# Banded attention of a streaming-encoder block: groups of 32 queries in place of transposes of the probabilities

## The reference, cut to what matters

```python
x = x + 0.5 * swiglu(rms_norm(x, ff1_norm), ...)          # d_ff 2816
proj = rms_norm(x, mix_norm) @ w_in                       # q 8 heads x 64, k and v 2 heads x 64, u 512
# attention: chunk n (64 queries) sees keys of chunks n-1 and n (128 keys)
scores = q @ k_win.T * 64 ** -0.5 - slope[head] * |qi - kj|
m = max(max(scores), sink[head])
p = exp(scores - m);  p = p / (sum(p) + exp(sink[head] - m))
attn = p @ v_win
ssm = s5_ssm_glu(u, ...)                                  # state space group, GELU, GLU
x = x + concat(rms_norm(attn), rms_norm(ssm)) @ w_out
x = x + 0.5 * swiglu(rms_norm(x, ff2_norm), ...);  out = rms_norm(x, final_norm)
```

## Time and profile before

| what | value |
|---|---|
| median of 3 runs (lowest, highest) | 1579.27 us (1579.03, 1579.45) |
| the profiled execution's own time | 1579.26 us |
| its span in the trace | 1577.6 us |
| mean granted TensorE clock | 0.999 |
| PE, DVE, ACT, POOL busy | 1568.1, 1104.8, 708.1, 533.0 us |

### The profile page before, as it was taken

One profiled execution on the slowest core, in us unless ns is written; L12 is line 12 of the kernel. 1 busy time (PEld: TensorE's weight loads), 2 busy tenths in 40 slices (PEclk: granted clock), 3 DMA queues, 4 the chain that ended last, 5 costly groups with the idle time before them and its releaser, 6 DMA issues.

```text
span 1577.6 us, 21967 instructions
## 1 busy us (share of the span) xinstructions
PE 1568.1 (99%) x7481; PEld 1295.2 (82%) x7481; DVE 1104.8 (70%) x1740; ACT 708.1 (45%) x1305; POOL 533.0 (34%) x986
## 2 busy tenths in 40 slices
PE   9999999999999999999999999999999999999998
PEld 7888888888888888878887888888888888888887
DVE  7966677666579887864368768765666666588767
ACT  7543434343434445421567544444444434344444
POOL 4228888877567778323130240000000000002000
PEclk9999999999999999999999999999999999999999
DMA  8363334333488555777631141333333333886444
GB/s 289 97 85 111 109 130 139 131 134 135 154 322 266 153 136 138 222 227 177 137 120 41 54 160 50 111 107 108 107 107 107 107 107 129 315 276 180 121 111 170
DMA packets 164311, 231.89 MB, mean 147 GB/s; under 512 B 26856, under 2 KB 100464, under 8 KB 160752
## 3 DMA queue, kind: packets, MB, share of 16 engines
q1 hardware_dynamic: 159728, 222.07, 44.2%
q0 software_dynamic: 4320, 8.41, 3.0%
q10 hardware_dynamic: 160, 0.07, 0.0%
HBM read 154.26 MB, written 75.20 MB: 145 GB/s over the span
## 4 chain that ended last, share of the span: by engine, by line
PE 99%; DMA 0%; ACT 0%; issue 0%; DVE 0%; SPq 0%; DVEq 0%; ACTq 0%
PE bank L1209 31%; PE bank L1211 31%; PE bank L1210 31%; PE bank L1552 1%; PE bank L1579 1%; PE bank L1534 1%; PE bank L1505 0%; PE bank L1565 0%; PE bank L1527 0%; DMA x_in<-in_x_dram 0%; PE bank L1243 0%; PE bank L1427 0%; PE bank L1235 0%; PE bank L1431 0%; PE bank L1428 0%; PE bank L1714 0%
## 5 line engine op out<-in xcount | busy, mean ns | idle before, releaser
L1209 PE MATMUL bank<-hbhi,ws_lo 128*128 128x512 f32 x1040 | 405.1, 390 | 0.0
L1211 PE MATMUL bank<-hbhi,ws_hi 128*128 128x512 f32 x1040 | 404.7, 389 | 0.0
L1210 PE MATMUL bank<-hblo,ws_hi 128*128 128x512 f32 x1040 | 404.6, 389 | 0.0
L1211 PEld LDWEIGHTS bank<-hbhi,ws_hi 128*128 128x128 f32 x1040 | 195.2, 188 | 40.9
L1209 PEld LDWEIGHTS bank<-hbhi,ws_lo 128*128 128x128 f32 x1040 | 195.2, 188 | 40.7 <-issue 0.4
L1210 PEld LDWEIGHTS bank<-hblo,ws_hi 128*128 128x128 f32 x1040 | 195.2, 188 | 40.2
L1209 PE MATMUL bank<-d_hi,ws_lo 128*128 128x512 f32 x572 | 222.7, 389 | 0.0
L1211 PE MATMUL bank<-d_hi,ws_hi 128*128 128x512 f32 x572 | 222.5, 389 | 0.0
L1210 PE MATMUL bank<-d_lo,ws_hi 128*128 128x512 f32 x572 | 222.5, 389 | 0.0
L1836 ACT ACTIVATE loc<-bank 128x512 f32<-128x512 f32 x160 | 96.0, 600 | 252.0 <-PE bank L1211 252.0
L1883 ACT ACTIVATE d_hi<-d_in 128x512 fp32r<-128x512 f32 x154 | 96.5, 631 | 202.6 <-DMA d_in<-b_scratch 202.5
(11 more groups left out here) (320 smaller groups left out, 2710.7 us busy)
## 6 DMA issues: line engine op xcount, KB each, us to landing
b_scratch<-loc SPq DMA_DIRECT2D x42, 1024.0 KB, 7.3
d_in<-b_scratch SPq DMA_DIRECT2D x154, 256.0 KB, 3.4
raw2a<-in_ff_w_up_dram SPq DMA_DIRECT2D x42, 512.0 KB, 4.8
loc<-in_ff_w_gate_dram SPq DMA_DIRECT2D x36, 512.0 KB, 5.1
xT<-x_scratch SPq DMA_DIRECT2D x12, 1024.0 KB, 7.7
x_scratch<-xT SPq DMA_DIRECT2D x5, 2048.0 KB, 8.1
dw_lo_place<-in_ff_w_down_dram SPq DMA_DIRECT2D x8, 1024.0 KB, 7.3
x_in<-in_x_dram SPq DMA_DIRECT2D x8, 512.0 KB, 7.8
```

The lines of the kernel that those rows point to most:

```text
L1209: nc.tensor.matmul(o, wl, rh, start=first, stop=False, skip_group_check=chain)
L1210: nc.tensor.matmul(o, wh, rl, start=False, stop=False, skip_group_check=chain)
L1211: return nc.tensor.matmul(o, wh, rh, start=False, stop=last, skip_group_check=chain)
```

## The change

- The partition axis of scores and probabilities is now four groups of 32 queries, one per chunk: a step m takes four chunks and half of the heads. `S` has 32 matmuls (64 rows, 32 columns, 128 keys moving), eight in a round: four column groups times two row halves.
- The sink is column 129 of each row of `sco`, written by POOL before the scores (`set_sinks`). The maximum runs over 129 columns, and so do the exponentials and their sums; the sink's own instructions are gone on DVE and ACT.
- `B` is the reciprocal alone. POOL multiplies by it (128x1024). `t` on DVE transposes the blocks of 32x32 into one buffer `pts` (two instructions of 128x512). T and C are gone.
- `V` has 32 matmuls: 32 keys (four row groups, one per chunk), 64 columns (two column groups, one per key/value head), 128 moving columns, four accumulated products each; chunk a goes to bank 2 + a. `O` copies from four banks in one instruction.
- `sco` has three buffers, numbered in the semaphore counts by `sinks_number` (m + 1 up to m = 2, then 2m - 1) and `scaled_number` (2m + 4 up to m = 5, then m + 9). The p steps have two banks in place of three. The order tables are rewritten; V7 stands right ahead of n0, which now waits for O7, and n1 stands behind p15.
- v goes through DRAM: 4 DMAs into `vt_scratch`, a wait on the SP queue, 16 DMAs into `vwin`. The bias is loaded by 16 DMAs behind the four `xT` loads, where one DMA in the state-space part loaded it.
- The injection I2 moves from projection (7, 1) to the start of projection (8, 0), nine matmuls of 128x512 later.

The diff, cut to what the text speaks of:

```diff
 WITH_PE = {(1, 1): steps("m1"), (6, 0): steps("K0"), (6, 1): steps("I0"),
-           (7, 0): steps("I1"), (7, 1): steps("I2"),
+           (7, 0): steps("I1"), (8, 0): steps("I2"),
            (10, 0): steps("Y0 I3"), (10, 1): steps("Y1"), (11, 1): steps("Y2"), (12, 0): steps("Y3")}
...
-ATT_PE = steps("P0 P1 S2 p2 T0 p3 T1 V0 S3 p4 V1 S4 T2 p5 T3 V2 S5 p6 V3 S6 p7 T4 p8 T5 V4 S7 p9 V5 p10 T6 p11 T7 V6 V7 p12 n0 p13 r0 p14 n1 p15")
-ATT_ACT = steps("W13 X0 X1 C0 C1 O0 X2 X3 O1 C2 W14 C3 O2 X4 O3 X5 W15 C4 C5 O4 X6 s0 s1 X7 O5 C6 s2 s3 q0 C7 O6 W16 O7 s4 s5 s6 s7 n0 W17 h0 h1 h2 h3 n1 W18 h4 h5 h6 h7 W19")
-ATT_DVE = steps("A0 A1 B0 p0 p1 B1 A2 W13 A3 B2 p2 p3 B3 p4 A4 W14 p5 A5 p6 B4 p7 B5 A6 W15 p8 A7 B6 p9 B7 p10 a0 W16 p11 j5 g0 j6 n0 j7 p12 W17 p13 h0 h1 h2 h3 p14 g1 p15 W18 n1 h4 h5 h6 h7 W19")
+ATT_PE = steps("P0 P1 p2 S2 p3 S3 p4 V0 S4 p5 V1 S5 p6 V2 p7 S6 V3 p8 S7 V4 p9 p10 V5 p11 V6 p12 V7 n0 p13 p14 r0 p15 n1")
+ATT_ACT = steps("W13 W14 X0 X1 X2 O0 W15 X3 O1 X4 O2 X5 O3 s0 X6 O4 X7 W16 s1 O5 s2 W17 O6 s3 O7 q0 n0 s4 s5 s6 s7 h0 h1 h2 h3 n1 W18 h4 h5 h6 h7 W19")
+ATT_DVE = steps("W13 A0 p0 A1 p1 W14 B0 p2 A2 t0 B1 A3 B2 p3 t1 A4 p4 B3 p5 t2 A5 t3 B4 p6 p7 A6 t4 B5 p8 A7 B6 t5 W15 p9 B7 p10 t6 W16 t7 p11 a0 p12 g0 W17 n0 j5 p13 j6 p14 h0 h1 j7 h2 h3 g1 p15 n1 W18 h4 h5 h6 h7 W19")
...
-SSM_BANK = [6, 7, 5]
-V_BANK = [4] * 7 + [0]
+SSM_BANK = [7, 6]
+V_BANK = [2, 3, 4, 5]
...
+def sinks_number(m):
+
+    return m + 1 if m < 3 else 2 * m - 1
+
+
+def scaled_number(m):
+
+    return 2 * m + 4 if m < 6 else m + 9
...
-    nm = small("nm", [P, 2, 8])
-    esk = small("esk", [P, 2, 8])
-    ssum = small("ssum", [P, 2, 8])
-    rden = small("rden", [P, 8])
...
             sp.wait_ge(pads_set, 1)
-            vt = vTp[:, :].rearrange("p (n c i) -> p n c i", c=2, i=32)
-            for c in range(4):
+            for d in range(4):
+                sp.dma_start(vt_d[:, :, 32 * d:32 * d + 32].rearrange("n j i -> j n i"),
+                             vTp[32 * d:32 * d + 32, :].rearrange("j (n i) -> j n i", i=32)).then_inc(v_loaded, 16)
+            sp.wait_ge(v_loaded, 4 * 16)
+            for a in range(4):
+                for n in range(4):
+                    c = 8 * n + 2 * a
+                    sp.dma_start(vwin[32 * a:32 * a + 32, n, :, :],
+                                 vt_d[c:c + 4, :, :].rearrange("b j d -> j b d")).then_inc(v_loaded, 16)
+
+        def load_bias():
+            sp.wait_ge(glu_done, 8)
+            sp.wait_ge(y_ready, 8)
+            for b in range(4):
                 for a in range(4):
-                    sp.dma_start(vwin[32 * c:32 * c + 32, :, 32 * a:32 * a + 32],
-                                 vt[32 * a:32 * a + 32, c // 2:c // 2 + 16, c % 2, :]).then_inc(v_loaded, 16)
+                    sp.dma_start(biast[32 * a:32 * a + 32, b, :, :, :].rearrange("p v g k -> p (v g k)"),
+                                 bias_c[32 * b:32 * b + 32].rearrange("i v k -> i (v k)")).then_inc(side_loaded, 16)
 
...
                 if h:
-                    pe.wait_ge(mix_taken, 14)
+                    pe.wait_ge(mix_taken, 15)
                 else:
-                    pe.wait_ge(pt_taken, 16)
+                    pe.wait_ge(o_taken, 8)
             elif norm == N_FF2 and h == 0:
...
                 pe.wait_ge(pads_set, 1)
-            for nn in range(2):
-                n = 2 * m + nn
-                for a in range(2):
+            for gl in range(2):
+                for qh in range(2):
+                    for a in range(4):
+                        n = 4 * (m // 2) + a
+                        for kv in range(NKV):
+                            r = slice(kv * HD, (kv + 1) * HD)
+                            o = bank[kv][32 * a:32 * a + 32, (2 * gl + qh) * P:(2 * gl + qh + 1) * P]
+                            last = nc.tensor.matmul(o, qT[r, n, 2 * (m % 2) + gl, 32 * qh:32 * qh + 32],
+                                                    kTp[r, n * CHUNK:n * CHUNK + P], start=True, stop=True,
+                                                    skip_group_check=True)
+                            if gl == qh == 1 and a == 3:
+                                last.then_inc(s_ready, 1)
+
+        def weighted(m):
+            if m:
+                pe.wait_ge(o_taken, m)
+            else:
+                pe.wait_ge(v_loaded, 20 * 16)
+                pe.wait_ge(h_tmp, split_before(N_ATT))
+            pe.wait_ge(p_turned, 2 * m + 2)
+            for b in range(4):
+                for a in range(4):
+                    k = slice(32 * a, 32 * a + 32)
                     for kv in range(NKV):
-                        r = slice(kv * HD, (kv + 1) * HD)
-                        o = bank[kv][:, (2 * nn + a) * P:(2 * nn + a + 1) * P]
-                        last = nc.tensor.matmul(o, qT[r, n, 2 * a:2 * a + 2, :].rearrange("p g q -> p (g q)"),
-                                                kTp[r, n * CHUNK:n * CHUNK + P], start=True, stop=True)
-                        if nn == a == 1:
-                            last.then_inc(s_ready, 1)
-
-        def transposes_p(m):
-            pe.wait_ge(p_done, m + 1)
-            if m:
-                pe.wait_ge(pt_taken, 2 * m)
-            for kv in range(NKV):
-                for nn in range(2):
-                    for a in range(2):
-                        o = bank[2 + kv][:, (2 * nn + a) * P:(2 * nn + a + 1) * P]
-                        last = nc.tensor.transpose(o, sco[m % 2][:, kv, nn, a, :], ident[:, :])
-                last.then_inc(pt_ready, 1)
-
-        def weighted(m):
-            if m == 7:
-                pe.wait_ge(s_biased, 16)
-            elif m:
-                pe.wait_ge(o_taken, m)
-            else:
-                pe.wait_ge(v_loaded, 16 * 16)
-                pe.wait_ge(h_tmp, split_before(N_ATT))
-            pe.wait_ge(pt_taken, 2 * m + 2)
-            for nn in range(2):
-                for kv in range(NKV):
-                    last = nc.tensor.matmul(bank[V_BANK[m]][kv * HD:(kv + 1) * HD, nn * 256:(nn + 1) * 256],
-                                            vwin[:, 2 * m + nn, kv * HD:(kv + 1) * HD],
-                                            pts[m % 2][:, kv, nn, :, :].rearrange("p a q -> p (a q)"),
-                                            start=True, stop=True)
+                        d = slice(kv * HD, (kv + 1) * HD)
+                        last = nc.tensor.matmul(bank[V_BANK[a]][d, 0:P], vwin[k, m // 2, b, d],
+                                                pts[k, kv, :, b, :], start=b == 0, stop=b == 3,
+                                                skip_group_check=True)
             last.then_inc(o_ready, 1)
 
         def ssm_piece(i, between=None):
...
             act.wait_ge(max_done, m + 1)
-            for s in range(8):
-                kv, nn, a = s // 4, s // 2 % 2, s % 2
-                v = sco[m % 2][:, kv, nn, a, :]
-                act.activation(v, v, ACT.Exp, bias=nm[:, m % 2, s:s + 1], scale=1.0,
-                               accum_out=ssum[:, m % 2, s:s + 1])
-            act.activation(esk[:, m % 2, :], esk[:, m % 2, :], ACT.Exp).then_inc(exp_done, 1)
-
-        def p_out(m):
-            for kv in range(NKV):
-                act.wait_ge(pt_ready, 2 * m + kv + 1)
-                if m >= 2:
-                    act.wait_ge(o_ready, m - 1)
-                else:
-                    act.wait_ge(h_tmp, split_before(N_ATT))
-                act.activation(pts[m % 2][:, kv, :, :, :].rearrange("p n a q -> p (n a q)"), bank[2 + kv][:, :],
-                               ACT.Copy).then_inc(pt_taken, 1)
+            for c in range(8):
+                v = sco[m % 3][:, c, :]
+                last = act.activation(v, v, ACT.Exp, bias=nm[:, m % 3, c:c + 1], scale=1.0,
+                                      accum_out=ssum[:, m % 3, c:c + 1])
+            last.then_inc(exp_done, 1)
 
         def o_out(m):
 
             act.wait_ge(o_ready, m + 1)
-            act.activation(qT[:, 2 * m:2 * m + 2, :, :].rearrange("p n g q -> p (n g q)"), bank[V_BANK[m]][:, :], ACT.Copy
-                           ).then_inc(o_taken, 1)
+            n = 4 * (m // 2)
+            act.activation(qT[:, n:n + 4, 2 * (m % 2):2 * (m % 2) + 2, :].rearrange("p n g q -> p n (g q)"),
+                           banks[:, V_BANK[0]:V_BANK[3] + 1, 0:P], ACT.Copy).then_inc(o_taken, 1)
 
...
+                dve.wait_ge(side_loaded, 16 * 16)
+                dve.wait_ge(p_done, sinks_number(2))
+            if m >= 3:
+                dve.wait_ge(p_turned, 2 * m - 4)
+                dve.wait_ge(p_done, sinks_number(m))
             for kv in range(NKV):
                 dve.wait_ge(s_ready, 2 * m + 2)
-                dve.scalar_tensor_tensor(sco[m % 2][:, kv, :, :, :].rearrange("p n a k -> p n (a k)"),
-                                         bank[kv][:, :].rearrange("p (n k) -> p n k", n=2), HD ** -0.5,
-                                         biast[:, kv, :].unsqueeze(1).to_broadcast([P, 2, 256]),
```

(48 more changed lines are left out.)

66 lines of the change are left out of this document (32 added, 34 removed).

## The result

| kernel | median, us (lowest to highest) | ratio to before, 95% interval |
|---|---|---|
| before | 1578.95 (1578.18 to 1580.37, 20 runs) | |
| changed | 1580.61 (1579.54 to 1584.35, 20 runs) | 1.0014 [1.0008, 1.0021] |

The change makes the kernel 1.7 us slower, by an interval (0.08% to 0.21%, 1.3 to 3.3 us) that leaves out no change but is hardly wider than the 0.2% that the prediction called undecidable. The forecast was 5.0 us faster, with a range up to 1579.0; it was wrong.

A forecast was written before the change was run, and what follows sets the result against it. PE was taken to bound the kernel (busy 1568.1 of 1577.6 us), so only time off PE's list or gaps counts. Terms -7.3 + 0.8 + 0.3 + 0.9 - 1.2 + 1.5 = -5.0 gave 1574.3 us, range 1571.9 to 1579.0.

The forecast's parts named there:

- I2: Injection moved behind nine matmuls: PE's 1.15 us wait for the last `u8` load goes, -1.2 us (bounds 0 to 1.2).
- glu(4): PE's GLU step waits for its bank because unit loads come 3.4 us late against 1.9 slack: +1.5 us (0 to 5.8).
- T goes: Attention on PE: the eight T steps, 0.82 to 0.96 us each, disappear, -7.3 us.
- S keeps its time: Scores on PE: four times the matmuls with a quarter of the columns, eight tiles at a time; 0 us.
- V changes shape: Attention on PE: each V becomes 64 records in 8 rounds of 128 columns, +0.1 us each, +0.8 in all.
- edges: Small steps stand between PE's pieces in 12 places instead of 10, at 0.15 us a place: +0.3 us.
- The rival with serial row groups: V's row groups run one after another: +2.7 us each, +21 in all, 1596 us; chance 0.08.
- n0 behind O7: End of attention: n0 directly follows V7 and waits for O7's bank, so PE stands: +0.9 us (0.6 to 1.1).
- v through DRAM: SP queue: four stores, a wait, then 16 loads make units 10 and 11 3.4 us late; +1.5 us.
- three p steps to hide under, as before: Work behind n0 (spread, scaled halves) stays hidden under three p steps; no cost added.
- GpSimd's product: Attention's 128x1024 product takes 2.6 to 4.5 us; PE waits for nothing up to about 4.2, so 0 us.
- The rival that it binds: GpSimd's product above 4.2 us delays V5 to V7: 1576.0 us at 4.5, 1583 at 5.5; chance 0.10.

The follow-up runs named there:

- sinks_pairs: Changed kernel with the sink table loaded as before (eight DMAs of 64 partitions, neighbouring values) and spread by GpSimd; 1576.24 us, 0.9991.
- before_sinks: Kernel before with the changed kernel's eight sink loads into a table of their own, copied by VectorE into the old table; 1583.25 us, 1.0031.
- sinks_gap: sinks_pairs with each load (64 partitions) writing every second value, as the changed kernel does; 1576.19 us, 0.9984.
- sinks_wide: sinks_pairs with eight sink loads of 128 partitions, neighbouring values, each quarter of the table loaded twice; 1575.85 us, 0.9984.
- late_windows: Changed kernel with the loads of units 10 and 11 issued between the four v stores and the wait for them, ahead of the window loads; 1579.01 us, 1.0001.
- i2_old: Changed kernel with the injection I2 back inside projection (7, 1); 1581.30 us, 1.0014.
- before_i2: Kernel before with only the injection I2 moved to the start of the next projection; 1578.20 us, 0.9996.
- combined_3: combined_2 with VectorE's h0 and h1 (scaled halves of the attention output) moved ahead of p14's take; 1573.87 us, 0.9969.
- combined_2: combined with W17, which waits for a weight load, moved behind O7 on ACT; 1574.80 us, 0.9974.
- combined: Changed kernel with sinks_pairs, late_windows and a new order of the last steps (V5 to V7 and r0 earlier) together; 1580.13 us, 1.0007.
- vt_last: Changed kernel with the DRAM tensor for v declared behind all others, so scratch tensors keep their old places; 1580.26 us, 1.0009.

## Why the prediction was wrong, point by point

**The step that failed: a term that was left out.** The prediction looked at PE in the attention part and at "whoever feeds PE at the places whose order changes". So it costed what the change does from 700 us on, and among the DMAs that it moves only those on SP. That the sink becomes a column of `sco` also gave its table another layout, and so other loads: eight DMAs on GpSimd's queue at 32 to 37 us, which stand in the diff and in no term of the sum. They cost 3.3 to 4.4 us (sinks_pairs, before_sinks), by holding the DMA engines while a store of the first feed-forward part needs them: it landed in 10.0 us instead of 3.0. This step alone turns the sign: without it the changed kernel is at 1576.24 us, 2.6 under the 1578.84 beside it (1.4 by the ratio, whose interval ends at 1.0000), faster and in the range. sinks_gap and sinks_wide, whose loads do not delay the store either, stand at 0.9984 with intervals that end below 1.

**The sum for the rest.** The table above gives sinks_pairs' profile 3.2 us under before at the last step, where the sum had 5.0 less. (The base of the sum was right: 1579.27 against 1578.95 of 20 runs.) Even without the sinks the kernel gains some 2 us less than forecast; the terms that were too good are those at I3, glu(4), attention and the tail. Term by term, from the same table:

| term | forecast | measured (sinks_pairs) |
|---|---|---|
| I2, K0 to Y0 | -1.2 | -1.5 |
| I3, Y0 to Y1 | 0 | +0.45 |
| glu(4), Y1 to the norm sums | +1.5 | +1.8 (idle 1.5, and a slower restart) |
| attention, S0 to n0: T, V, edges, n0 | -5.3 | -4.9 |
| n0 to the second r | 0 | +0.7 |
| sinks | none | +4.2 in the medians, +3.3 by the ratios |

- *T goes, S keeps its time, V changes shape, edges*: right. V is 1.13 to 1.14 where 1.12 was forecast, S 1.09. The rival with serial row groups (+2.7 a V) is out. The 0.4 between -5.3 and -4.9 is not traced to one term.
- *n0 behind O7*: 0.78 idle and a little restart against 0.9. Right.
- *v through DRAM*: the loads 3.1 us late against 3.4, the gap 1.56 against 1.5; late_windows shows the cause. Of its parts, the stores took longer to issue (0.97 each, forecast 0.67 to 0.9), landed 2.6 us behind the last issue, and the loads were just under the lower bound of 0.48, 7.43 / 16 = 0.46. What the sum did not have is the restart: the stretch is 1.8 us longer for an idle time of 1.5, and in i2_old the lower clock behind this gap costs another 1.7.
- *I2*: -1.5 in sinks_pairs' profile, not to be told from none in the medians. The changed kernel's own profile shows 0.6 of it, with 0.84 idle at I1. What was missed is who is next: I3 waits for the last `u8` loads. That PE meets them because it is 1.2 us earlier is argued and not shown: before_i2 has the same move and no gap there, before_sinks keeps I2's old place and has 0.20.
- *n0 to the projection*: the step that failed here is "three p steps to hide under, as before". There are three, but r0 and VectorE's first h steps stand behind p14 now, so one p and n1 are left between r0 and the attention half, where p14, n1 and p15 were; GpSimd's hT_lo comes 0.48 us late. combined_3 shows that r0 and the first h steps ahead of p14 take it away; r0 alone, in combined_2, did not.
- *GpSimd's product*: 1.90 us, below the range of 2.6 to 4.5. The rival that it binds is out, and the 2.26 us of a 128x512 product beside VectorE was no guide to it. Why it is so quick stays open.

## What to carry to other kernels

List every DMA that a change touches, on every queue and at whatever time it runs, and not only those near the code that the change is about: here eight transfers of 1 KB each cost more than the 2.6 us that the changed kernel gains without them. A step moved earlier on one engine gains only if the lists of all engines that feed it let it: look in each of these lists for a step that stands ahead and waits for something unrelated (a weight load, a PE step). When single terms come out as forecast and the time does not, lay the starts of the same steps of both traces side by side; the first row in which they part names the place.

## What the runs showed of the hardware

- Tiny loads on GpSimd's queue can hold up a store of another queue: with eight loads of 128 partitions x 2 values (4 bytes each, 8 bytes apart) the packets of that queue took 30.3% of 16 engines over 20 us (49.8% from 45 to 50), and a 512 KB store of SP landed in 10.0 us instead of 3.0. With 64 partitions (1.2%) or neighbouring values (8.0%) the store was not delayed. The Trainium skill ("DMA: Bandwidth & Descriptors", section "Rules for kernel authors") says that a strided last dimension becomes one descriptor per element. In these runs such a last dimension was harmless at 64 partitions and harmful at 128.
- Four row groups of 32 rows with two column groups, accumulating into four banks, ran 64 records of 128 columns in 1.13 us (V in the changed kernel).
- ACT copied from four banks (128 columns of each) in 0.60 us, the time of a copy of 512 columns from one (0.60).
- Behind a stop of PE of 4.12 us the granted clock was 0.83 over 870 to 880 us (combined), and the same 0.83 stands behind stops of 2.1 to 2.2 us in vt_last, late_windows and i2_old. Behind stops of 2.2 us in the changed kernel's two profiles and in before_sinks it stayed at 1.00. So one and the same gap can cost 1.7 us more in one execution than in the next.
